# Linear attention's eight score levels merged by predicated copies, the experts' tokens fetched by indirect transfer, and three rotating weight slots

## The reference, cut to what matters

```
def step(s, blk):
    qc, kc, vc, gc = blk
    G = jnp.cumsum(gc, axis=2)
    decay = jnp.exp(jnp.where(tri, G[:, :, :, None, :] - G[:, :, None, :, :], -jnp.inf))
    scores = jnp.einsum('bhik,bhjk,bhijk->bhij', qc, kc, decay)
    o = jnp.einsum('bhij,bhjv->bhiv', scores, vc) + jnp.einsum('bhik,bhkv->bhiv', qc * jnp.exp(G), s)
    ...
```

```
def moe_swiglu(x, w_router, w_gate, w_up, w_down):
    logits = (x @ w_router).astype(jnp.float32)
    top_v, top_i = lax.top_k(logits, TOP_K)
    top_w = jax.nn.softmax(top_v, axis=-1)
    gates = jnp.sum(jax.nn.one_hot(top_i, N_EXPERTS, dtype=jnp.float32) * top_w[..., None], axis=-2)
    out = jnp.zeros_like(x)
    for e in range(N_EXPERTS):
        out = out + gates[..., e:e + 1].astype(x.dtype) * swiglu(x, w_gate[e], w_up[e], w_down[e])
    return out
```

## Time and profile before

| what | value |
|---|---|
| runs | 3308.59 us median of 3 (3307.46 to 3311.27) |
| profiled execution, own time | 3307.04 us |
| its span in the trace | 3305.2 us, clock share 0.971 |
| pairs: first scores to the next stage's first product | 310.28 to 439.18 us |
| experts: first gate product to the last down product | 2284.0 to 3239.8 us, 8 passes |

### The profile page before, as it was taken

The page is one execution under the profiler, slowest core; times in us unless marked ns, Lnnn a source line. Parts: engine busy times, 40 slices in busy tenths (PEclk is TensorE's granted clock), DMA queues, the critical chain, the costliest instruction groups (busy, mean ns, idle before and its releaser), DMA issues.

```text
span 3305.2 us, 41618 instructions
## 1 busy us (share of the span) xinstructions
PE 3089.6 (93%) x18128; PEld 1757.4 (53%) x18128; DVE 802.9 (24%) x1629; ACT 411.6 (12%) x1012; POOL 333.7 (10%) x376
## 2 busy tenths in 40 slices
PE   6989789999999999989998999998999999999997
PEld 2456544444447777657755777454444444444443
DVE  1136943000034766610033000243000000000002
ACT  1014211000012222110012000130000000000001
POOL 1122720000001332310000000000000000000030
PEclk9989988999999999989989999998999999999998
DMA  8670001312112122143443333326899999999992
GB/s 349 246 277 2 1 1 64 114 64 78 69 45 67 45 65 65 70 162 119 153 166 115 134 134 136 128 77 249 342 395 369 358 378 390 357 361 404 360 380 84
DMA packets 210612, 609.13 MB, mean 184 GB/s; under 512 B 6076, under 2 KB 53404, under 8 KB 203904
## 3 DMA queue, kind: packets, MB, share of 16 engines
q1 hardware_dynamic: 204912, 592.20, 47.2%
q0 software_dynamic: 5056, 13.67, 1.2%
q10 hardware_dynamic: 464, 0.60, 0.1%
HBM read 600.28 MB, written 6.16 MB: 183 GB/s over the span
## 4 chain that ended last, share of the span: by engine, by line
PE 84%; DVE 9%; issue 3%; DMA 2%; ACT 2%; POOL 1%; POOLq 0%; ACTq 0%; DVEq 0%
PE ps_ffn_gate L610 10%; PE ps_ffn_up L610 10%; PE ps_ffn_down L646 10%; PE ps_moe_down L3020 6%; PE ps_moe_gate L2975 6%; PE ps_moe_up L2975 6%; PE ps_odd L1929 4%; PE ps_lin L1409 4%; PE ps_project L528 3%; PE ps_moe_down L3026 3%; PE ps_moe_up L2980 3%; PE ps_moe_gate L2980 3%; PE ps_lin L296 3%; PE ps_ple_gate L2602 2%; DVE rec_qd L2188 2%
## 5 line engine op out<-in xcount | busy, mean ns | idle before, releaser
L610 PE MATMUL ps_ffn_gate<-hT,ring_buf 128*128 128x256 f32 (+1 forms) x1152 | 343.6, 452 | 4.3 <-issue 2.3
L610 PE MATMUL ps_ffn_up<-hT,ring_buf 128*128 128x256 f32 (+1 forms) x1152 | 336.7, 445 | 1.3
L646 PE MATMUL ps_ffn_down<-ring_buf,ffn_hiddenT 128*128 128x512 f32 x752 | 325.9, 593 | 3.0 <-issue 3.0
L610 PEld LDWEIGHTS ps_ffn_gate<-hT,ring_buf 128*128 128x128 f32 x1152 | 222.0, 194 | 120.5 <-issue 99.1
L610 PEld LDWEIGHTS ps_ffn_up<-hT,ring_buf 128*128 128x128 f32 x1152 | 217.9, 190 | 110.3 <-issue 90.0
L1929 PE MATMUL ps_odd<-ring_buf,hT 128*128 128x256 f32 (+2 forms) x1024 | 236.1, 385 | 8.0 <-ACT hg_kT L2064 6.4
L646 PEld LDWEIGHTS ps_ffn_down<-ring_buf,ffn_hiddenT 128*128 128x128 f32 x752 | 141.7, 190 | 182.0 <-issue 181.9
L695 DVE TENSOR_TENSOR ffn_hiddenT<-ffn_silu_buf,ps_ffn_up 128x256 f32<-128x256 f32 (+1 forms) x72 | 36.2, 503 | 727.4 <-PE ps_ffn_up L610 727.4
L3152 DVE TENSOR_TENSOR moe_hidden_buf<-moe_silu_buf,ps_moe_up 128x768 f32<-128x768 f32 (+1 forms) x32 | 27.3, 855 | 747.2 <-PE ps_moe_up L2980 747.2
L1929 PEld LDWEIGHTS ps_odd<-ring_buf,hT 128*128 128x128 f32 x1024 | 173.7, 192 | 55.1 <-ACT hg_kT L2064 7.9
L2975 PE MATMUL ps_moe_up<-ring_buf,moe_xg_buf 128*64 128x512 f32 (+1 forms) x1024 | 199.5, 542 | 0.3 <-DMA ring_buf<-in_w_exp_up_dram 0.3
(11 more groups left out here) (508 smaller groups left out, 3495.3 us busy)
## 6 DMA issues: line engine op xcount, KB each, us to landing
ring_buf<-in_w_exp_up_dram SPq DMA_DIRECT2D x24, 4096.0 KB, 16.7
ring_buf<-in_w_exp_down_dram SPq DMA_DIRECT2D x24, 4096.0 KB, 16.3
moe_third<-in_w_exp_gate_dram SPq DMA_DIRECT2D x16, 4096.0 KB, 18.0
mod_pieces<-in_mod_w_dram SPq DMA_DIRECT2D x40, 1024.0 KB, 6.5
ring_buf<-in_w_exp_gate_dram SPq DMA_DIRECT2D x8, 4096.0 KB, 17.5
ring_buf<-in_odd_w_in_dram SPq DMA_DIRECT2D x40, 512.0 KB, 5.3
moe_third<-in_w_exp_gate_dram SPq DMA_DIRECT2D x8, 2048.0 KB, 11.0
ring_buf<-in_w_exp_up_dram SPq DMA_DIRECT2D x8, 2048.0 KB, 7.8
```

What stands on the lines that cost most here:

```text
L610: mm = nc.tensor.matmul(ps[:, 0:wide], view[:, k, i * P:(i + 1) * P], hT[:, k, first_col:first_col + wide], start=k == 0, stop=k == KD - 1)
L646: mm = nc.tensor.matmul(ps_y[i % 2][:, h, :], hidT[:, b, i * P:(i + 1) * P], view[:, b, h * 512:(h + 1) * 512], start=first, stop=end)
```

## The change

Three edits, each on its own engine lists. In the pairs the masks are no longer multiplied into 8 levels and added up: two "places" a head take levels 0 and 1 times their masks, and three predicated copies lay levels 2 and 3, 4 and 5, 6 and 7 over them where their masks are set (the masks are disjoint); each waits for the one before. `halves` and `add_levels` are gone, and PE multiplies both places by the values, four products and not two. In the experts, DVE makes `pick` for the next pass at a pass's start, PE turns it into 96 row numbers (`numbers`, after gate 0), DVE copies them to SBUF, POOL fetches the rows by an indirect DMA from a copy of the tokens in DRAM (`moe_tokens`, written once, row 0 zero), and `gather` is eight transposes of what came. The last gate and up piece (2 MB each) share one slot, so that a pass has 11 items, and the slots rotate from pass to pass.

```diff
+    for j in range(2):
+        c[:, C_MISC + 60 + j] = 1 + j * P + i
...
-            masked = tail(1, 0, 2 * NL * P).rearrange("p (e l n) -> p e l n", e=2, l=NL)
+            merged = tail(1, 0, 2 * 2 * PLACES * P).rearrange("p (b e s n) -> p b e s n", b=2, e=2, s=PLACES)
...
-                    pe.wait_ge(S["rec_summed"].handle, S["rec_summed"].at(u + 1))
+                    pe.wait_ge(S["rec_masked"].handle, S["rec_masked"].at(u + 1))
...
-                        mm = nc.tensor.matmul(ps_out[:, e, :], summed[:, u % 2, e, :], vs(u, e), start=fresh(u),
-                                              stop=fresh(u) or e == 1)
+                        for s in range(PLACES):
+                            mm = nc.tensor.matmul(ps_out[:, e, :], merged[:, u % 2, e, s, :], vs(u, e),
+                                                  start=fresh(u) and s == 0,
+                                                  stop=s == PLACES - 1 and (fresh(u) or e == 1))
...
-                def halves(u):
-                    for e in range(2):
-                        pool.wait_ge(S["rec_masked"].handle, S["rec_masked"].at(2 * u + e + 1))
-                        nc.gpsimd.tensor_tensor(masked[:, e, 0:4, :], masked[:, e, 0:4, :], masked[:, e, 4:8, :],
-                                                ALU.add).then_inc(S["rec_halved"].handle, 1)
...
-                for u in range(n):
-                    halves(u)
-                    if u + 2 < n:
-                        keys(u + 2)
-                    if u == n - 2:
-                        root(1, 0, 4, slice(0, 2))
-                        root(2, 0, 2, slice(2, 4))
+                for u in range(2, n):
+                    keys(u)
+                root(1, 0, 4, slice(0, 2))
+                root(2, 0, 2, slice(2, 4))
...
-                def mask(u):
+                def merge(u):
+
+                    d, mine = units[u][1], merged[:, u % 2, :, :, :]
                     dve.wait_ge(S["rec_scores"].handle, S["rec_scores"].at(u + 1))
-                    dve.wait_ge(S["rec_summed"].handle, S["rec_summed"].at(u))
-                    for e in range(2):
-                        nc.vector.tensor_tensor(masked[:, e, :, :], ps_scores[:, e, :, :], T.mask[:, units[u][1], :, :],
-                                                ALU.mult).then_inc(S["rec_masked"].handle, 1)
-
-                def add_levels(u):
-                    dve.wait_ge(S["rec_halved"].handle, S["rec_halved"].at(2 * u + 2))
                     if u >= 2:
                         dve.wait_ge(S["rec_out"].handle, S["rec_out"].at(u - 1))
-                    nc.vector.tensor_reduce(summed[:, u % 2, :, :], masked[:, :, 0:4, :].rearrange("p e l n -> p e n l"),
-                                            AX.X, ALU.add).then_inc(S["rec_summed"].handle, 1)
+                    for r in range(ROUNDS):
+                        levels = slice(r * PLACES, (r + 1) * PLACES)
+                        made_by = ps_scores[:, :, levels, :]
+                        which = T.mask[:, d, levels, :].unsqueeze(1).to_broadcast([P, 2, PLACES, P])
+                        if r == 0:
+                            last = nc.vector.tensor_tensor(mine, made_by, which, ALU.mult)
+                        else:
+                            last = nc.vector.copy_predicated(mine, which.bitcast(I32), made_by)
+                        if r < ROUNDS - 1:
+                            link_v(last)
+                    last.then_inc(S["rec_masked"].handle, 1)
...
-                    mask(u)
+                    merge(u)
                     if u + 2 < n:
                         queries(u + 2)
                     if u >= 1:
                         take(u - 1)
-                    if u == n - 1:
-                        gated(0, (0, 1), 1)
-                    add_levels(u)
-                gated(0, (2, 3), 1)
+                gated(0, range(4), 1)
...
-    UP_ITEM = [1] + [3 * c for c in range(1, NP)]
-    DOWN_ITEM = [3 * c + 4 for c in range(NP - 1)] + [3 * NP - 1]
+    UP_ITEM = [1] + [3 * c for c in range(1, NP - 1)] + [GATE_ITEM[NP - 1]]
+    DOWN_ITEM = [3 * c + 4 for c in range(NP - 2)] + [3 * NP - 3, 3 * NP - 2]
+    SHARED = GATE_ITEM[NP - 1]
+    ITEMS = 3 * NP - 1
...
+    def slot_of(item, p):
+        return (item + ITEMS * fixed_of(p)) % 3
...
+            rows_in = flat_ring[0:ROOM, 2 * BIG + 4 * D:2 * BIG + 5 * D]
+            number_of = const[:, C_MISC + 60:C_MISC + 62]
+            ps_number = ps_t[0:ROOM, KD - 1, P - 1:P]
...
-                        f = moe_free[item % 3]
+                    def fetch(item, rows, width, src, second=False):
+                        f = moe_free[slot_of(item, p)]
...
-                        sp.wait_ge(f.handle, f.at(item // 3) + p * NP)
-                        sp.dma_start(room_of(item, rows, width), src).then_inc(moe_loaded[item % 3], 16)
+                        sp.wait_ge(f.handle, f.at(0) + uses_before(item, p))
+                        sp.dma_start(room_of(item, p, rows, width, second), src)\
+                            .then_inc(moe_second_loaded if second else moe_loaded[slot_of(item, p)], 16)
...
+                def numbers(p):
+                    pe.wait_ge(S["moe_pick"].handle, S["moe_pick"].at(1) + p)
+                    for i in range(2):
+                        mm = nc.tensor.matmul(ps_number, pick[:, i, :], number_of[:, i:i + 1],
+                                              start=i == 0, stop=i == 1)
+                    mm.then_inc(S["moe_number"].handle, 1)
+
+                def gather(p):
+                    pe.wait_ge(moe_fetched, 16 * p)
+                    for k in range(KD):
+                        mm = nc.tensor.transpose(ps_t[:, k, 0:ROOM], rows_in[:, k * P:(k + 1) * P],
+                                                 ident[0:ROOM, 0:ROOM])
+                    mm.then_inc(S["moe_gather"].handle, 1)
+
...
                     gate(p, n0, 0)
+                    numbers(p + 1)
                     up(p, n0, 0)
...
-                    dve.wait_ge(S["moe_gather"].handle, S["moe_gather"].at(0) + p)
+                    if isinstance(p, int) and p == 1:
+                        dve.wait_ge(S["moe_gather"].handle, S["moe_gather"].at(1))
+                    else:
+                        dve.wait_ge(S["moe_number"].handle, S["moe_number"].at(-1) + p)
...
+                    dve.wait_ge(S["moe_number"].handle, S["moe_number"].at(0) + p)
+                    nc.vector.tensor_copy(token[:, :], ps_number).then_inc(S["moe_number_taken"].handle, 1)
...
+                    choose(p + 1)
                     if not isinstance(p, int):
                         choose_back(p)
                     for c in range(NP):
-                        hidden(n0, c)
-                        if c == NP - 2:
-                            choose(p + 1)
...
+                load(pool, "pool", (moe_tokens[1:1 + 2 * P, :].rearrange("(t p) n -> p t n", p=P), X[:, 2:4, :]))
+
+                def one_pass(p):
+                    pool.wait_ge(S["moe_number_taken"].handle, S["moe_number_taken"].at(1) + p)
+                    if not isinstance(p, int):
+                        pool.sem_inc(S["moe_number_seen"].handle, 1)
+                    nc.gpsimd.indirect_dma_start(rows_in, None, moe_tokens[:, :],
+                                                 bass.IndirectOffsetOnAxis(ap=token[:, 0:1], axis=0))\
+                        .then_inc(moe_fetched, 16)
+                first_passes(one_pass)
                 n_passes = passes(pool)
+                other_passes(pool, n_passes, one_pass)
...
```

84 lines of the change are left out of this document (52 added, 32 removed).

## The result

The changed kernel takes 3253.60 us (median of 4 runs, 3248.43 to 3254.76), before it is 3308.03 us: 54.4 us less. The ratio over all runs is 0.9828, 95% interval [0.9816, 0.984]; the quotient of these two medians, 0.9836, lies inside it. The forecast was 3265 us with a range from 3256 to 3282: the direction and most of the mechanisms held, and the time lies 2.4 us under the range. The profiled execution took 3252.44 us, 1.16 under the median, with a span of 3250.4 us.

A forecast was written before the change was run, and what follows sets the result against it. DVE was taken to bound the pairs, with PE not far behind, and PE the experts, with DMA not far behind. 3307.04 less 25 (pairs) less 17.5 (experts) gave 3264.5, stated as 3265 us, range 3256 to 3282.

The forecast's parts named there:

- PE becomes the bound of the pairs, DVE is second: Pairs: PE's unit of 6.2 us would exceed DVE's new 5.4, where DVE had set 7.6.
- Merge 2.85 us: Pairs, DVE: one product and three predicated copies at 0.69 us each, plus 0.09 for chain waits.
- two rivals: Pairs: a copy of 512 takes 1.22 us (3278.5 us, chance 0.13), or 3.3 like the reciprocal (3380 us, 0.04).
- Query product near 1.2 us once `halves` are gone: Pairs, DVE: the product takes 1.1 to 1.2 us alone, and 1.1 more was waiting for POOL.
- second rival: Pairs: copies wait for POOL's keys, merge 4.2 us, DVE's unit 6.7 and still the bound; 3274 us, chance 0.15.
- Experts -17.5: Experts: transposes replace the gather's products, numbers cost 0.45 us; net -2.2 us a pass over eight passes, bounds -7.5 and -19.
- Without the shared slot each pass waits 1.2 us: Experts: with a shorter gather PE would wait 1.2 us a pass for down 2; the slot's cover is worth 10 us.
- I go nearer that end: -22.: Pairs, scores: -25 us at full clock, -16 if the clock stays 0.90; -22 taken, nearer full clock.
- Sum 6.2 us: Pairs, PE's unit: scores 2.0, sums and rest 2.2, output 1.5, two more products by the values 0.55 us.
- Where 114 are now: Pairs: first to last scores take 114 us before the change (116 less last hand-off and mask start), 89 after.
- The tail: End of the pairs, 13.2 us before: loses reduction and halves, gains 0.5 of merge and four moved `gated`; -3 us.
- The ring at the end: nothing.: After the experts: next stage's loads wait 6.5 us more for PE's last product, yet land before they are wanted; no cost.

The follow-up runs named there:

- one and by four places: Changed kernel with one merged place instead of two: 3258.58 us, ratio 0.9853; with four instead of two: 3261.78 us, ratio 0.9853.
- the changed kernel with waits: Changed kernel with 368 more long-fulfilled waits ahead of PE's first product, making PE's program as long as before: 3258.05 us, ratio 0.9848.
- the run with doubled copies: Changed kernel with each predicated copy made twice, the second writing the same values again: 3292.01 us, ratio 0.9948.
- the second execution: Changed kernel, unchanged, profiled once more: 3255.00 us.

## Why the prediction was wrong by 11 us

The steps that held, each with its measured size:

- *PE becomes the bound of the pairs, DVE is second.* Shown by one and by four places.
- *Merge 2.85 us:* 2.97. The copy costs 737 ns, near its lower bound of 0.69, far from the 1.22 and 3.3 of two rivals. *DVE's unit 5.4 us:* 5.44 from one `pair_total` to the next (350.28 to 355.72), with no wait between.
- *Query product near 1.2 us once `halves` are gone:* 1.22 in the timeline. *The copies wait for the keys* (second rival) fell: in the timeline the first copy runs beside the keys, and all 48 take 722 to 752 ns. The Trainium skill, page "SBUF — State Buffer", section "Who interferes with whom", lets a VectorE instruction with at most one SBUF input, outside the two-port modes, run free of GpSimd; the trace agrees, and the copy's own destination doesn't count as a second one.
- *Experts -17.5:* -17.1. The nearness is partly luck. A pass fell by 2.50 us (forecast 2.2), since eight transposes take 0.81 us and not 1.07 (the numbers 0.43, forecast 0.45), which makes 20 us in eight. Two things not in the sum took 2.9 us back. The first pass's gate products took 8.78 us where they took 7.09: a lower clock, in both profiles of the changed kernel and with the pairs' edit alone, but not with the experts' edits alone nor in the changed kernel with waits, so it isn't tied to the experts' edits. And in the last pass PE waits 2.4 us for loads (1.0 and 1.4), before 1.2. The forecast had named late loads in the last pass as a danger and given them no price; whether they collide with the final row fetches, as it said, no run shows. *Without the shared slot each pass waits 1.2 us:* 1.4, 10.6 us in the time (forecast 10).

The steps that failed:

1. *"I go nearer that end: -22."* The mechanism (PE idles less, so the clock comes back) was right, and the run with doubled copies shows it; but the clock is full, not nearly so. The discount took 3 us from the 25 that the same sum gives at full clock.
2. *"Sum 6.2 us", PE's unit.* A regular unit is 5.81 us, and with no waiting. Added up were lengths of groups, which overlap at their seams; from start to start the parts are 1.98 for the scores, 2.05 for the sums and 1.78 for the output, where the sum had 2.0, 2.2 and 2.05. Over 16 units that is 6 us too many, but only 2.3 came out: from the first scores to the end of the last it is 86.7 us (310.50 to 397.22), forecast 89. The rest was hidden by a second error, so that is luck. The forecast took 6.6 us off for the three units without sums, as if PE bounded them too. There DVE bounds: in the two steps at the end PE waits 1.8 and 1.3 us for it, and they take 5.80 and 5.32 us and not 4.0.
3. *"Where 114 are now".* To the end of the last scores it was 115.4 us (310.28 to 425.72), which adds 1.4. The pairs so gave 28.7 us up to there and not 22: 3.0 by the clock, 2.3 by the unit, 1.4 by the start of the reckoning. The tail, forecast at -3, gave -3.5.
4. *"The ring at the end: nothing."* The next stage's loads come later and are hidden, as said. The stall behind the last down product wasn't seen: 3.0 us, and 0.9 by the clock behind it. It stood in the trace, as 5.15 us of `issue`. In the changed kernel two things work against it: the loads held back by the ring, which alone left 0.55 us of it in the kernel before, and the other place of PE's code, which alone is enough; the pairs' edit alone, with the old ring and full DMA engines, has lost the stall too.

And 1.9 us in the conditioning products behind the pairs: the sum had nothing for them, and they went back to half clock in the second execution.

Together 6.7 + 0.5 + 3.9 + 1.9 = 13.0 us, less 0.4 for the experts and 0.2 because the pairs start that much later: 12.4, where the spans differ from the sum of the prediction by 54.8 - 42.5 = 12.3. (The forecast of 3265 lies 11.4 above the measured median: the profiled execution of the changed kernel is 1.16 us quicker than its median.) The range was too narrow at its low end, since the discounted clock and the overcounted unit lay on the same side, and the stall beside them.

## What to carry to other kernels

Take the length of a unit from start to start of the same instruction, not as a sum of groups: the seams overlap, here by 0.4 us in 6. Then ask for every shorter unit anew which engine bounds it: a unit with less for PE was not shorter here, because DVE's 5.4 us stayed. Where an edit takes PE from waiting to working, reckon with the full clock and take the discount into the range alone: the pairs ran at 1.00 in every profile in which PE was busy 94% of them or more. Look for idle time with the releaser "issue" and ask the DMA view for the instruction queue in that window: a block of code behind a loop may be waiting behind a load that nobody needs yet, and holding that load back cost nothing here, where its data were wanted 21 us after its later issue.
